# Splitting each 128x520 output tile of a hybrid decoder layer into a pass of high weights and a pass of low weights

## The chip, the cores and the metric

The kernel runs on one core of a Trainium2 chip. The metric is device time in microseconds (us) of one execution, the median of several runs. TensorE (PE) multiplies, with its weight loads told apart as PEld; VectorE is DVE, ScalarE ACT, GpSimd POOL; SyncE (SP) issues most of the transfers.

## The reference, cut to what matters

One decoder layer is computed for 512 prompt tokens and 8 sample tokens together (520 columns), with a final norm. Nearly all the work is nine matrix products in float32:

```python
z = xn @ w_in                       # q, k, v, o, ig, fg, u, vb, ga, gb
y_a = (jax.nn.sigmoid(o) * h) @ w_a
y_b = spatial_gate(u, vn, w_s, b_s) @ w_b
x = x + (jax.nn.sigmoid(ga) * y_a + jax.nn.sigmoid(gb) * y_b) @ w_o
up = rmsnorm(x, g2) @ w_up          # then a causal convolution of width 3
x = x + (jax.nn.silu(a) * gval) @ w_down
```

## The kernel before, in words

**Split products.** A float32 weight W is split into a high part (`whi`, rounded by ACT into the type float32r) and a low part (`wlo` = W - whi, by DVE), and so is each activation (`xh`, `xl`). A product W x is then three products: whi xh, whi xl and wlo xh.

**Slots and tiles.** The weights come in 149 slots of 128x1024 (those of the last product, `w_down`, of 128x1024 or 128x896). Slot by slot, SP loads into `raw` (two buffers), ACT's `split` (its activations all have line 427) makes `whi` and raises `w_hi`, DVE's `low` (line 748) makes `wlo` and raises `w_lo`. `whi` and `wlo` have two buffers each; ACT takes one again when the tile that read it has raised `done`. On PE one call of `tile` (lines 1318 to 1338) works through a slot: 8 k tiles (7 in some of `w_down`), and for each the three products for both column halves of 260: 6 matmuls a k tile, 48 a tile. The matmul itself is line 1316 (`MM`). The two halves lie in the two banks of `out_ps[p]`, which is emptied (`evac`) by ACT or DVE before the tile after next may begin. The last slot group (output tile 7 of `w_down`, 132 matmuls) isn't done by `tile` but by `last_tile` (line 1502), half by half.

**What a tile waits for.** At its start: `w_lo` of its slot, and the emptied bank. Four tiles also have `each`: before the products of k tile k they wait until k+1 tiles of their activation have been made. These are `S_GATE` (the gates, on `s_xu`, from DVE line 770), `S_Q` (on `s_xn`, DVE line 791), `S_WO` (the first tile of w_o, on `s_m`, from DVE line 1077: `ml`) and `S_UP` (the first of w_up, on `s_x2`, DVE line 1090: `x2l`). In `S_WO` and `S_UP` the eighth activation tile comes out of the tile of PE that ran just before: ACT or DVE read its bank, DVE makes the next `wlo`, a high part is made by ACT and the low part by DVE.

**Work in the middle of a tile.** `mid` is called after the products of k tile `mid_at`; it issues transposes, or the products of another part, or sums over partitions. Those that the prediction speaks of are `square_sums` (lines 1351 to 1356, in slot `S_VB + 1`, `mid_at=0`), whose sum leads through ACT's square root and DVE's reciprocal (line 786) to `scaled_vb` (line 799), which empties the bank for `S_VB + 2`; and `norm_sums` (lines 1474 to 1479, in `S_UP`, `mid_at=5`), which takes POOL's sums of squares (lines 1290 to 1294).

The rule of order in the four `each` tiles stands in these lines:

```python
for k in range(nk):
    if each is not None:
        pe.wait_ge(each, k + 1)
```

Of the kernel before, what the change touches and what calls it, by code (L numbers as in the profile page):

```python
# [23 lines left out]
P = 128  # L24
# [5 lines left out]
HALF = TOK // 2  # L30
# [47 lines left out]
def hybrid_layer(nc, ins, outs):  # L78
    with ExitStack() as ctx:
# [5 lines left out]
        def at(name, shape, offset, dt=F32):  # L85

            return nc.alloc_sbuf_tensor_at(name, shape, dt, offset=base + offset)
# [4 lines left out]
        def sem(name):  # L92
            return ctx.enter_context(nc.semaphore(name))
# [70 lines left out]
        whi = [at(f"whi{t}", [P, KT * P], R0 + 8192 + 4096 * t, F32R) for t in range(2)]  # L164
        wlo = [at(f"wlo{t}", [P, KT * P], R0 + 16384 + 4096 * t, F32R) for t in range(2)]
# [101 lines left out]
        w_hi = sem("w_hi")  # L267
        w_lo = sem("w_lo")
# [1045 lines left out]
        def _(pe):  # L1314
            def MM(*a, **k):
                return pe.matmul(*a, **k)  # L1316

            def tile(n, hi, lo, k0=0, nk=KT, bank=None, use=None, start=True, stop=True, mid=None, mid_at=3, each=None, end=None):

                p = n.c % 2  # L1320
                pe.wait_ge(w_lo, n(1))
                if start:
                    pe.wait_ge(evac[p if bank is None else bank], n.half(1) if use is None else use)
                o = out_ps[p if bank is None else bank]
                for k in range(nk):
                    if each is not None:
                        pe.wait_ge(each, k + 1)
                    w = slice(k * P, (k + 1) * P)
                    for wt, x in ((whi[p], hi), (whi[p], lo), (wlo[p], hi)):
                        for a in range(2):  # L1330
                            m = MM(o[:, a, 0:HALF], wt[:, w], x[:, k0 + k, a * HALF:(a + 1) * HALF],
                                   start=start and k == 0 and wt is whi[p] and x is hi,
                                   stop=stop and k == nk - 1 and wt is wlo[p])
                    if k == mid_at and mid is not None:
                        mid()
                m.then_inc(done, 1)
                if end is not None:
                    end()

            def transposes(b, evn, vb=None):  # L1340

                if vb is None:
                    evacuated(pe, evn)
                else:
                    pe.wait_ge(s_vbg, vb + 1)
                pe.wait_ge(tre[b.c % 2], b.half(1))
                for c in range(NC):
                    m = pe.transpose(trp[b.c % 2][:, c, :], ftmp[b.c % 2][:, c * P:(c + 1) * P], ident[:, :])  # L1348
                m.then_inc(tr_done, 1)
# [13 lines left out]
            for _ in range(WARM):  # L1363
                MM(aux[:, 0, 0:P], ones[:, :], ones[:, :], start=True, stop=True)
            tile(At(S_GATE), xuh, xul, each=s_xu)
            tile(At(S_VB), xuh, xul)
            tile(At(S_VB + 1), xuh, xul, mid_at=0, mid=square_sums)
            pe.wait_ge(s_tri, 1)
            tile(At(S_VB + 2), xuh, xul, mid_at=4, mid=lambda: vb_transposes(0), end=lambda: vb_transposes(1))
# [59 lines left out]
            with pe.Fori(1, 4) as i:  # L1429
                for t in range(2):  # L1430
                    tile(At(S_V + t, i, 2), xh, xl,
                         mid=lambda: transposes(At(B_V + t - 1, i, 2), At(S_V + t - 1, i, 2)))
# [182 lines left out]
```

## Time and profile before

| | us |
|---|---|
| median of 3 runs (lowest, highest) | 921.11 (920.89, 921.35) |
| the profiled execution | 922.31 |
| its span in the trace | 919.8 |
| PE busy in the span | 905.6 (98%) |
| PE weight loads busy | 900.7 (98%) |
| DVE busy | 529.1 (58%) |
| ACT busy | 365.1 (40%) |
| POOL busy | 135.6 (15%) |

The span is what the trace covers; the device time of the same execution is 2.5 us longer. Busy times of PE count a matmul from its start to its modelled end, and matmuls overlap, so the pace of PE is read from the starts of rows and their counts, not from the mean of one. In the timeline a row that says x2 is two matmuls (the two column halves), and its start is that of the first.

### The profile page before, as it was taken

To read this page: it belongs to the slowest core of one execution; us is meant where nothing else is said; L and a number is where in the kernel's file an instruction comes from. 1 tells how busy PE (TensorE), PEld (TensorE's weight loads), DVE (VectorE), ACT (ScalarE), POOL (GpSimd) and SP (SyncE) were. 2 spreads that over 40 slices of the span, in tenths; PEclk is the share of its full clock that TensorE was granted. 3 is DMA by queue.
4 is the path that set the end of the run, shared out by engine and by line. 5 is a ranking of instruction groups with operands and counts; after the bars stand their busy time and mean duration, and the time that the engine had idled before them with its cause. 6 is when DMAs were issued, how large, how long until landed. Compare 5 with 4: busy or idle time off the path is not lost.

```text
span 919.8 us, 19638 instructions
## 1 busy us (share of the span) xinstructions
PE 905.6 (98%) x7442; PEld 900.7 (98%) x7442; DVE 529.1 (58%) x811; ACT 365.1 (40%) x553; POOL 135.6 (15%) x182
## 2 busy tenths in 40 slices
PE   9999999999999999999999999999999999999995
PEld 9999999999999999999999999999999999999995
DVE  7877565443884444333346777777777777323235
ACT  7653334544863323222223344444444444222231
POOL 0871000002541111000016500000000000000002
PEclk9999999999999999999999999999999999999998
DMA  5332432234862222532233222222222222332322
GB/s 208 109 99 93 138 137 102 85 101 156 300 249 69 69 74 86 175 100 91 91 111 81 93 87 92 91 91 91 91 91 91 91 91 90 103 94 86 97 69 93
DMA packets 30187, 100.21 MB, mean 109 GB/s; under 512 B 4524, under 2 KB 6604, under 8 KB 29896
## 3 DMA queue, kind: packets, MB, share of 16 engines
q1 hardware_dynamic: 28672, 93.99, 30.7%
q0 software_dynamic: 1328, 5.72, 2.3%
q8 instruction: 24, 0.39, 0.2%
q14 instruction: 11, 0.09, 0.0%
q10 hardware_dynamic: 152, 0.02, 0.0%
HBM read 92.37 MB, written 7.35 MB: 108 GB/s over the span
## 4 chain that ended last, share of the span: by engine, by line
PE 92%; POOLq 3%; issue 2%; DVE 1%; DMA 1%; POOL 1%; ACT 0%; DVEq 0%; SPq 0%; ACTq 0%
PE out L1316 86%; PE aux L1316 2%; PE trp L1316 2%; POOLq L1293 2%; POOLq L1291 1%; PE trp L1348 1%; DMA raw<-in_w_dn 0%; PE aux L1454 0%; DMA cwb<-in_conv_wb 0%; DVE y L1177 0%; POOL out_conv_old L1277 0%; DVE ftmp L1173 0%; POOLq L1284 0%; DVE wlo L748 0%; POOL sconv L1285 0%
## 5 line engine op out<-in xcount | busy, mean ns | idle before, releaser
L748 DVE TENSOR_TENSOR wlo<-raw,whi 128x1024 fp32r<-128x1024 f32 (+1 forms) x148 | 188.4, 1273 | 207.5 <-ACT whi L427 207.2
L427 ACT ACTIVATE whi<-raw 128x1024 fp32r<-128x1024 f32 (+1 forms) x148 | 155.4, 1050 | 253.0 <-PE out L1316 251.3
L1316 PE MATMUL out<-xh,whi 128*128 128x260 f32 x768 | 158.7, 288 | 0.0
L1316 PE MATMUL out<-xh,wlo 128*128 128x260 f32 x768 | 154.6, 283 | 0.0
L1316 PE MATMUL out<-xl,whi 128*128 128x260 f32 x768 | 154.3, 282 | 0.0
L1316 PE MATMUL out<-x2h,wlo 128*128 128x260 f32 x704 | 141.9, 283 | 0.0
L1316 PE MATMUL out<-x2h,whi 128*128 128x260 f32 x704 | 141.8, 282 | 0.0
L1316 PE MATMUL out<-x2l,whi 128*128 128x260 f32 x704 | 141.6, 283 | 0.0
L1316 PEld LDWEIGHTS out<-xh,whi 128*128 128x128 f32 x768 | 118.7, 189 | 0.5
L1316 PEld LDWEIGHTS out<-xh,wlo 128*128 128x128 f32 x768 | 118.3, 188 | 0.0
L1316 PEld LDWEIGHTS out<-xl,whi 128*128 128x128 f32 x768 | 118.2, 188 | 0.0
L1316 PEld LDWEIGHTS out<-x2h,whi 128*128 128x128 f32 x704 | 108.6, 188 | 0.1
L1316 PEld LDWEIGHTS out<-x2h,wlo 128*128 128x128 f32 x704 | 108.5, 188 | 0.0
L1316 PEld LDWEIGHTS out<-x2l,whi 128*128 128x128 f32 x704 | 108.2, 188 | 0.0
L1316 PE MATMUL out<-acth,whi 128*128 128x260 f32 x338 | 70.7, 283 | 1.6 <-DVE wlo L748 1.6
L1316 PE MATMUL out<-acth,wlo 128*128 128x260 f32 x338 | 70.6, 283 | 0.0
L1316 PE MATMUL out<-actl,whi 128*128 128x260 f32 x338 | 70.4, 283 | 0.0
L1112 DVE TENSOR_TENSOR up<-out,rbc 128x520 f32<-128x520 f32 x44 | 30.9, 701 | 42.3 <-PE out L1316 42.2
L1316 PEld LDWEIGHTS out<-acth,whi 128*128 128x128 f32 x338 | 53.1, 188 | 1.9 <-DVE wlo L748 1.8
L1316 PEld LDWEIGHTS out<-acth,wlo 128*128 128x128 f32 x338 | 53.1, 188 | 0.0
L1316 PEld LDWEIGHTS out<-actl,whi 128*128 128x128 f32 x338 | 53.0, 188 | 0.0
L1299 POOL COPY nconv<-up 128x10 f32 x44 | 8.9, 203 | 242.9 <-DVEq L1113 242.9
(266 smaller groups left out, 1397.9 us busy)
## 6 DMA issues: line engine op xcount, KB each, us to landing
raw<-in_w_slots SPq DMA_DIRECT2D x125, 512.0 KB, 3.3
raw<-in_w_dn SPq DMA_DIRECT2D x16, 448.0 KB, 3.3
c_ring<-in_C_state SPq DMA_DIRECT2D x8, 512.0 KB, 4.6
row<-scratch SPq DMA_DIRECT2D x8, 512.0 KB, 5.5
out_C_sample<-c_ring SPq DMA_DIRECT2D x8, 512.0 KB, 4.2
raw<-in_w_dn SPq DMA_DIRECT2D x8, 512.0 KB, 3.5
x<-in_x_all SPq DMA_DIRECT2D x4, 520.0 KB, 6.2
xres<-in_x_all POOLq DMA_DIRECT2D x1, 2080.0 KB, 11.4
```

The lines of the kernel that those rows point to most:

```text
L427: return act.activation(out, in_, func, **kw_)
L748: TT(wlo[p][:, 0:width], raw[p][:, 0:width], whi[p][:, 0:width].bitcast(F32), ALU.subtract)\
L1112: TT(both(up[t][:, 2:2 + TOK]), out2(n), both(rbc2[:, :]), ALU.mult).then_inc(evac[n.c % 2], 1)
L1291: pool.drain()
L1293: pool.drain()
L1299: pool.tensor_copy(nconv[:, i * 2 + t, :], up[t][:, SEQ:2 + TOK]).then_inc(s_nc, 1)
L1316: return pe.matmul(*a, **k)
L1348: m = pe.transpose(trp[b.c % 2][:, c, :], ftmp[b.c % 2][:, c * P:(c + 1) * P], ident[:, :])
```

## The change

Inside `tile` the order is turned: the outer loop is now over the two weight parts, the inner over the k tiles. The first pass has 4 matmuls a k tile (whi with the high and the low activation), 32 in all, and carries the waits of `each`; the second has 2 a k tile (wlo with the high activation), 16 in all. The tile's start waits for `w_hi`, and `w_lo` is waited for ahead of the second pass. `mid` is called at the place in the new order that is nearest to where it was, by number of matmuls.

```diff
             def tile(n, hi, lo, k0=0, nk=KT, bank=None, use=None, start=True, stop=True, mid=None, mid_at=3, each=None, end=None):
 
                 p = n.c % 2
-                pe.wait_ge(w_lo, n(1))
+                pe.wait_ge(w_hi, n(1))
                 if start:
                     pe.wait_ge(evac[p if bank is None else bank], n.half(1) if use is None else use)
                 o = out_ps[p if bank is None else bank]
-                for k in range(nk):
-                    if each is not None:
-                        pe.wait_ge(each, k + 1)
-                    w = slice(k * P, (k + 1) * P)
-                    for wt, x in ((whi[p], hi), (whi[p], lo), (wlo[p], hi)):
-                        for a in range(2):
-                            m = MM(o[:, a, 0:HALF], wt[:, w], x[:, k0 + k, a * HALF:(a + 1) * HALF],
-                                   start=start and k == 0 and wt is whi[p] and x is hi,
-                                   stop=stop and k == nk - 1 and wt is wlo[p])
-                    if k == mid_at and mid is not None:
-                        mid()
+                for q, wt in enumerate((whi[p], wlo[p])):
+                    if q == 1:
+                        pe.wait_ge(w_lo, n(1))
+                    for k in range(nk):
+                        if each is not None and q == 0:
+                            pe.wait_ge(each, k + 1)
+                        w = slice(k * P, (k + 1) * P)
+                        for x in ((hi, lo), (hi,))[q]:
+                            for a in range(2):
+                                m = MM(o[:, a, 0:HALF], wt[:, w], x[:, k0 + k, a * HALF:(a + 1) * HALF],
+                                       start=start and q == 0 and k == 0 and x is hi,
+                                       stop=stop and q == 1 and k == nk - 1)
+                        if mid is not None and (q, k) == (((0, (3 * mid_at + 2) // 2), (1, 3 * mid_at + 2 - 2 * nk))[3 * mid_at + 2 >= 2 * nk]):
+                            mid()
                 m.then_inc(done, 1)
```

How the instructions move is shown at two places on PE. The first is the end of `S_WO`, the first tile of w_o, where `mh` and `ml` are the high and low parts of the merged branches and `merged_lo` is the semaphore that `ml` raises. Before:

```order
L1316 MATMUL out1<-mh_62,whi1_113 128x260 [waits merged_lo]
L1316 MATMUL out1<-mh_62,whi1_113 128x260
L1316 MATMUL out1<-ml_63,whi1_113 128x260 x2
L1316 MATMUL out1<-mh_62,wlo1_115 128x260 x2
L1316 MATMUL out0<-mh_62,whi0_112 128x260 [waits bank_emptied0,w_lo]
```

Now:

```order
L1316 MATMUL out1<-mh_62,whi1_113 128x260 [waits merged_lo]
L1316 MATMUL out1<-mh_62,whi1_113 128x260
L1316 MATMUL out1<-ml_63,whi1_113 128x260 x2
L1316 MATMUL out1<-mh_62,wlo1_115 128x260 [waits w_lo]
L1316 MATMUL out1<-mh_62,wlo1_115 128x260 x15
L1316 MATMUL out0<-mh_62,whi0_112 128x260 [waits bank_emptied0,w_hi]
```

The wait for the eighth `ml` had 42 matmuls of the tile ahead of it and 6 behind; now it has 28 ahead and 20 behind. The same holds in the other `each` tiles.

The second place is the start of slot `S_VB + 1`, where `square_sums` issues two matmuls into `aux` for the sum of squares of x (`xsum`). Before:

```order
L1316 MATMUL out0<-xuh_57,whi0_112 128x260 [waits bank_emptied0,w_lo]
L1316 MATMUL out0<-xuh_57,whi0_112 128x260
L1316 MATMUL out0<-xul_58,whi0_112 128x260 x2
L1316 MATMUL out0<-xuh_57,wlo0_114 128x260 x2
L1316 MATMUL aux<-xsum_54,ones 128x260 [waits square_sum_ready]
```

Now:

```order
L1316 MATMUL out0<-xuh_57,whi0_112 128x260 [waits bank_emptied0,w_hi]
L1316 MATMUL out0<-xuh_57,whi0_112 128x260
L1316 MATMUL out0<-xul_58,whi0_112 128x260 x2
L1316 MATMUL out0<-xuh_57,whi0_112 128x260 x2
L1316 MATMUL out0<-xul_58,whi0_112 128x260 x2
L1316 MATMUL aux<-xsum_54,ones 128x260 [waits square_sum_ready]
```

The sums stood behind 6 matmuls of the tile and stand behind 8. (In `S_VB + 2` a transpose moves in the same way from behind 30 matmuls to behind 32; the other calls of `mid` keep their number.) DVE, ACT and SP keep their order of instructions throughout.

## Rows read from the trace of the kernel before

**Rows 1.** The page, busy times with their shares of the span.
```profile
span 919.8 us, 19638 instructions
...
PE 905.6 (98%) x7442; PEld 900.7 (98%) x7442; DVE 529.1 (58%) x811; ACT 365.1 (40%) x553; POOL 135.6 (15%) x182
```

**Rows 2.** The chain that ended last, in order of time: start, length, what.
```profile
384.68 92.29 PE out L1316 x768
...
901.90 6.12 PE out L1316 x51
```

**Rows 3.** Waits of PE: us in total, times, longest.
```profile
PE out L1316 <- DVE wlo L748: 1.6, 1, 1.6
...
PE out L1316 <- DVE ml L1077: 0.6, 1, 0.6
```

**Rows 4.** Timeline of PE in S_WO: start, length, operation [idle before <-releaser].
```profile
476.80 0.40 PE L1316 MATMUL out<-mh,whi 128*128 128x260 f32 x2
...
482.56 0.51 PE L1316 MATMUL out<-mh,whi 128*128 128x260 f32 x2 [0.56 <-DVE ml L1077]
482.90 0.40 PE L1316 MATMUL out<-ml,whi 128*128 128x260 f32 x2
...
483.39 0.41 PE L1316 MATMUL out<-mh,whi 128*128 128x260 f32 x2
```

**Rows 5.** Timeline of DVE in the same stretch.
```profile
481.12 1.39 DVE L1077 TENSOR_TENSOR ml<-merged,mh  x1 [0.92 <-ACT mh L427]
```

**Rows 6.** Timeline of PE in S_UP.
```profile
523.75 0.40 PE L1316 MATMUL out<-x2h,whi 128*128 128x260 f32 x2
...
528.29 1.15 PE L1316 MATMUL aux<-acc,ones 128*128 128x260 f32 x4
529.08 0.60 PE L1316 MATMUL out<-x2h,whi 128*128 128x260 f32 x2
...
530.72 0.40 PE L1316 MATMUL out<-x2h,whi 128*128 128x260 f32 x2
```

**Rows 7.** Timeline of DVE and POOL in the same stretch.
```profile
526.95 1.80 DVE L1090 SCALAR_TENSOR_TENSOR x2l<-x,gains,x2h  x1
...
534.78 0.70 DVE L1112 TENSOR_TENSOR up<-out,rbc 128x520 f32<-128x520 f32 x1
...
526.09 2.10 POOL L1292 TENSOR_TENSOR acc<-acc,sqa 128x520 f32<-128x520 f32 x1
```

**Rows 8.** Timeline around S_GATE, and the line of the xl tiles.
```profile
8.65 4.11 DVE L770 SCALAR_TENSOR_TENSOR xul<-x,gains,xuh 128x520 fp32r<-128x520 f32 x6
...
8.93 0.49 PE L1316 MATMUL out<-xuh,whi 128*128 128x260 f32 x2
...
L791 DVE SCALAR_TENSOR_TENSOR xl<-x,gains,xh x8: 758/1374/1804, 33.7 to 61.8; 128x520 fp32r<-128x520 f32 x8
```

**Rows 9.** Timeline of PE, ACT and DVE from square_sums to the start of S_VB + 2.
```profile
21.28 1.04 PE L1316 MATMUL aux<-xsum,ones 128*128 128x260 f32 x4
...
22.36 0.69 ACT L427 ACTIVATE rbc<-aux,eps 128x520 f32<-128x520 f32 x1 [0.48 <-PE aux L1316]
...
23.08 3.40 DVE L786 RECIPROCAL rbc<-rbc 128x520 f32<-128x520 f32 x1
26.58 1.53 DVE L799 TENSOR_TENSOR ftmp<-out,rbc 128x520 f32<-128x520 f32 x2
...
26.96 0.41 PE L1316 MATMUL out<-xuh,wlo 128*128 128x260 f32 x2
...
27.43 0.48 PE L1316 MATMUL out<-xuh,whi 128*128 128x260 f32 x2
```

**Rows 10.** Timeline of PE's weight loads in the warm-up, up to the first tile.
```profile
1.20 5.88 PEld L1316 LDWEIGHTS aux<-ones 128*128 128x128 f32 x31 [1.20 <-DVE ones L762]
...
6.89 2.09 PEld L1316 LDWEIGHTS aux<-ones 128*128 128x128 f32 x18
```

**Rows 11.** Windows: stretch, length, busy PE, PEld, DVE, ACT, POOL, granted clock, DMA share, GB/s.
```profile
894.00:898.00 4.00, 3.64 (x30) 3.64 (x31) 1.62 (x3) 2.75 (x4) 0.00 (x0) 1.00 0.00 0
```

## The prediction

> **What bounds the kernel now.** I read the page's busy times first, then the chain that ended last, then PE's waits, and then the timeline around each tile that waits for its activations. PE is busy for 905.6 of 919.8 us [rows 1], and the chain shows how evenly: 768 matmuls in 92.29 us, 120.2 ns each, over 16 whole tiles with all their starts and loop ends [rows 2]. So PE's issue order sets the time, and only two things can change it: the pace of a matmul, and the moments when PE stands still. Of the latter PE's waits hold few: 1.6 us for a `wlo` and 0.6 us for `ml` [rows 3]. In the timeline a wait costs somewhat more than its listed idle time, because the row behind it also starts late: in `S_WO` the pairs follow at 0.34 us instead of 0.24 once [rows 4].
>
> **What the change removes.** The wait for `w_lo` at a tile's start becomes one for `w_hi`, which comes earlier. That is worth something only where a tile's start was late on `wlo`. The one listed wait on `wlo`, 1.6 us, is near the end, in `last_tile`, which the change doesn't touch; its loads, splits and `done` counts keep their order, so it stays. The tiles before it show none. I take 0 us, with 0 also as the bound of the gain: the 16 tiles of [rows 2] begin without any loss. The number of matmuls and weight loads (7442 each [rows 1]) is unchanged, and DVE, ACT and SP issue what they issued.
>
> **What the change adds, one.** A wait for `w_lo` in the middle of each of 146 tiles. By then `wlo` has been there longer than it was at the tile's start before, so the wait itself is over. Whether a wait that is over breaks the flow between matmuls isn't shown for this place. Lower bound 0: the same kind of wait at the tile starts of [rows 2] costs nothing. Upper bound: what a real wait adds behind it, 0.10 us (0.34 less 0.24 [rows 4]), 146 times, 14.6 us. I take 0, since the tile start is the nearest row by far.
>
> **What it adds, two: the `each` tiles.** The eighth activation tile is needed after 28 matmuls instead of 42, that is 14 x 0.120 = 1.68 us sooner, and the second pass can't be used to cover for it, since it stands behind. I go through the four.
>
> `S_WO` starts at 476.80 and the next tile at 483.39 [rows 4]: 6.59 us for 48 matmuls that take 48 x 0.120 = 5.77, so 0.82 us are lost now. `ml` ends at 481.12 + 1.39 = 482.51 [rows 5], and that moment hangs on the end of the tile ahead of `S_WO` (its bank, its `wlo`, `mh`), not on `S_WO` itself. PE will be at the eighth k tile at 476.80 + 28 x 0.120 = 480.16 and stand until 482.56. Since it already stands now, all of the 14 matmuls add to it: **+1.68 us**. Bounds 1.4 to 2.0.
>
> `S_UP` starts at 523.75. Its last `x2l` runs from 526.95 to 528.75, stretched beside POOL's addition, which ends at 528.19 [rows 7]; so far PE needed it only after the norm sums, at about 530.0, and lost nothing to it. The new order needs it at 523.75 + 3.36 = 527.11. With the 0.05 us from the end of `ml` to the next start and the 0.10 us of restart, as in `S_WO`, PE goes on as if at 528.90: 1.79 us lost. What it loses now goes away in return: the tile takes 530.72 - 523.75 = 6.97 us [rows 6], of which 5.77 are its matmuls and 4 x 0.22 = 0.88 the sums, so 0.32 us go to the wait for POOL, and after a stand of 1.79 us POOL is long done. Net **+1.47 us**. The lower bound is 0.4, if `x2l` should come as quickly as the 0.75 us that POOL leaves it elsewhere (the shortest of the like operation `xl` took 0.758 [rows 8]); the upper bound is 1.8. The row itself is taken, because POOL and DVE both start from the same `x1` as before. Next in line is the reciprocal chain that frees the bank for the tile after next: it was done at 534.78 + 0.70 = 535.48 [rows 7] and needed at 530.72 + 5.77 = 536.49, 1.0 us of cover. The norm sums move with the stand (36 matmuls are ahead of them in both orders), so the cover stays.
>
> `S_GATE` starts at 8.93, right behind the warm-up, whose last weight load ends at 6.89 + 2.09 = 8.98 [rows 8, 10], so the earlier `w_hi` gives nothing. The six last `xul` end between 9.4 and 8.65 + 4.11 = 12.76, one each 0.68 us. Today PE takes 0.72 us a k tile and is behind them; in the first pass it takes 0.48 and overtakes them. It would be at the eighth at 8.93 + 3.36 = 12.29 and goes on as if at 12.76 + 0.15 = 12.91: **+0.62 us**, bounds 0.4 and 0.9 (several short stands instead of one).
>
> `S_Q` costs nothing: the last `xl` starts at 61.8 [rows 8] and none took over 1.8 us, and its k tile is needed at about 67.
>
> **What it adds, three: `mid` moved.** `square_sums` stands 2 matmuls later, 0.24 us. Behind it is a chain: ACT's root at 22.36, DVE's reciprocal from 23.08, `scaled_vb` from 26.58, and PE starts `S_VB + 2` at 27.43 although its pairs were due at 26.96 + 0.24 = 27.20 [rows 9]. So this chain ends last there already, by 0.23 us, and the shift goes through: **+0.21 us** (a little of it is hidden behind the `wlo` that DVE makes ahead of the reciprocal), bounds 0 and 0.3. The transpose in `S_VB + 2` comes 0.24 us later and nothing waits for it soon; 0, bounds 0 and 0.2.
>
> **Sum.** 1.68 + 1.47 + 0.62 + 0.21 = 3.98 us, on a span of 919.8 and an execution of 922.31, which gives 923.8 and 926.3. The profiled execution lies 1.2 us above the median of the runs, 921.11; carried over to that, 925.1 us, +0.43%. The likely case's own bounds are 2.2 (1.4 + 0.4 + 0.4 + 0) and 5.2 (2.0 + 1.8 + 0.9 + 0.3 + 0.2).
>
> **Rivals.** *A: the order itself makes matmuls faster (not slower than before).* If part of the 120.2 ns were paid for changing between high and low operands, the second pass, with `wlo` and the high activation alone, could run quicker. There are 6924 matmuls in `tile`, so 3.98 / 6924 = 0.57 ns less for each, 0.5% of the pace, is the point from which the change isn't slower; twice that gives 917 us. Against it: `last_tile` has yet another order (whi, whi, wlo in one half, always the same bank) and runs 51 matmuls in 6.12 us, 120.0 ns [rows 2]; the pace doesn't react to the order. The Trainium skill, TensorE: Matmul & The Clock Gate, Back-to-back issue gap, gives a matmul of N columns N / 2.4 + 2.5 ns, an estimate of 110.8 ns for 260; the trace has 120.2. Were the new order to reach that figure, 6924 x 9.4 ns = 65 us would go; nothing in the trace points to it.
>
> *B: the middle wait breaks the flow.* 146 times 0.10 us, 14.6 us: 939.7 us. Against it speaks that tile starts are free; for it only that no row shows the place itself.
>
> *C: the long stand in `S_WO` costs speed afterwards.* At the start PE's weight loads took 5.88 / 31 = 0.190 us each, and later 2.09 / 18 = 0.116 [rows 10]; that slow stretch cost 31 x 0.074 = 2.3 us. If a stand of 2.4 us brought it back, the time would be 927.4 us. After the stand of 1.6 us in `last_tile` the granted clock was 1.00, 2.4 GHz [rows 3, 11], and `S_UP`'s stand is about as short. A stand of 2.4 us doesn't occur in the trace. The Trainium skill, same page, Why this matters for your kernels, warns that a pause between matmul bursts sends the clock to its lower level if it is long enough; this would be that case, and no row here shows where it begins.
>
> *D: the stands are absorbed.* If `ml` and `x2l` came sooner than in the trace, or each stand only replaced another further on, under 1.8 us would be left: 922.5 us. Against it: after `S_UP` the chain is PE without a wait until `last_tile`, so nothing further on can give the time back.
>
> **Chances.** The sum 0.79; A 0.06; B 0.05; C 0.06; D 0.04. What a measurement of this kernel can tell from no change is 0.2%, 1.84 us. The sum, B and C are slower: 0.90. A lies half beyond the other edge and half within, D within: faster 0.03, same 0.07. The predicted time is the sum's, 925.1 us. The range takes the sum's bounds, 923.3 to 926.3, and reaches upward to take in C: 923.2 to 927.5; A, B and D are left out, 0.15.
>
> **What would show it.** PE's waits would name `ml` with about 2.2 us in place of 0.6, `x2l` with about 1.6 (new), and `xul` with some tenths (new); POOL's 0.3 would be gone; the `wlo` wait would stay at 1.6 in `last_tile` and appear in no tile. `S_WO` would take 8.3 us from its start to the next tile, `S_UP` 8.4. Matmuls would go on at 120.2 ns, in both passes and over the pass boundary. The prediction is wrong if the pace moves by over 0.5 ns, if the pass boundary shows a gap, or if the two stands together are under 1.5 us.

## The result, and the profile after

The changed kernel takes 923.99 us (median of 6 runs, 923.23 to 925.66) against 921.23 us (920.89 to 921.42): 1.003 times the time before, with a 95% interval of 1.002 to 1.004. That is 2.76 us more, slower, where 3.98 us more were forecast. The profiled execution took 924.2 us with a span of 922.3 us.

The page of the changed kernel, busy times, against [rows 1]:

```profile
span 922.3 us, 19638 instructions
...
PE 904.8 (98%) x7442; PEld 899.0 (97%) x7442; DVE 525.7 (57%) x811; ACT 365.2 (40%) x553; POOL 135.9 (15%) x182
```

The span grew by 2.5 us while PE's busy time fell by 0.8: the loss is idle time. The fall in busy time is no measure of the pace of the matmuls, because the warm-up matmuls alone took 7.01 us in this execution and 7.97 in that of the kernel before. PE's waits of the changed kernel (total, times, longest), against [rows 3]:

```profile
PE out L1316 <- DVE ml L1077: 2.2, 1, 2.2
PE out L1316 <- DVE x2l L1090: 1.5, 1, 1.5
PE out L1316 <- DVE wlo L748: 1.4, 1, 1.4
PE aux L1316 <- DVE ones L762: 1.2, 1, 1.2
PE aux L1316 <- ACT sqa L427: 0.5, 1, 0.5
PE out L1316 <- DVE ftmp L799: 0.3, 1, 0.3
PE out L1316 <- DVE xul L770: 0.3, 1, 0.3
```

The wait for `ml` has grown from 0.6 us to 2.2, and those for `x2l` and `xul` are new. The wait for `scaled_vb` (`ftmp`) has become long enough to be listed. The one for `wlo` is still the one in `last_tile`, and no other tile waits for a `wlo`, neither at its start nor in its middle.

The timeline of PE in `S_WO` (start, length, operation, idle before it), against [rows 4]:

```profile
477.11 0.41 PE L1316 MATMUL out<-mh,whi 128*128 128x260 f32 x2
...
482.83 0.51 PE L1316 MATMUL out<-mh,whi 128*128 128x260 f32 x2 [2.21 <-DVE ml L1077]
...
483.42 2.08 PE L1316 MATMUL out<-mh,wlo 128*128 128x260 f32 x16
485.34 0.41 PE L1316 MATMUL out<-mh,whi 128*128 128x260 f32 x2
```

DVE there, against [rows 5]:

```profile
481.43 1.35 DVE L1077 TENSOR_TENSOR ml<-merged,mh  x1 [0.91 <-ACT mh L427]
```

`ml` starts 4.32 us after the tile's start, as before (481.12 - 476.80), so it hangs on the tile ahead. The tile now takes 485.34 - 477.11 = 8.23 us instead of 6.59. All 16 matmuls of `wlo` stand behind the late part and can't cover for it.

PE in `S_UP`, against [rows 6], and DVE, against [rows 7]:

```profile
525.66 0.41 PE L1316 MATMUL out<-x2h,whi 128*128 128x260 f32 x2
...
530.70 0.51 PE L1316 MATMUL out<-x2h,whi 128*128 128x260 f32 x2 [1.52 <-DVE x2l L1090]
...
531.77 1.04 PE L1316 MATMUL aux<-acc,ones 128*128 128x260 f32 x4
...
534.09 0.41 PE L1316 MATMUL out<-x2h,whi 128*128 128x260 f32 x2
```

```profile
528.87 1.77 DVE L1090 SCALAR_TENSOR_TENSOR x2l<-x,gains,x2h  x1
```

8.43 us instead of 6.97, and the sums (`aux`) no longer wait for POOL. At the start of the kernel (PE, against [rows 8, 9]) there are several short stands in `S_GATE`, and `S_VB + 2` starts at 28.18 instead of 27.43. With the shorter warm-up PE began `S_GATE` at 7.96 instead of 8.93, and overtook `xul` the sooner:

```profile
7.96 0.49 PE L1316 MATMUL out<-xuh,whi 128*128 128x260 f32 x2
...
9.46 0.51 PE L1316 MATMUL out<-xuh,whi 128*128 128x260 f32 x2 [0.29 <-DVE xul L770]
...
12.81 0.51 PE L1316 MATMUL out<-xuh,whi 128*128 128x260 f32 x2
...
25.52 0.40 PE L1316 MATMUL out<-xul,whi 128*128 128x260 f32 x2
25.76 2.10 PE L1316 MATMUL out<-xuh,wlo 128*128 128x260 f32 x16
...
28.18 0.48 PE L1316 MATMUL out<-xuh,whi 128*128 128x260 f32 x2 [0.32 <-DVE ftmp L799]
```

The rows at 25.52 and 25.76 are the last pair of a first pass and the first pair of its second: they follow at 0.24 us, as pairs do inside a pass, so the wait for `w_lo` at this boundary leaves no gap.

Last, the chain in order of time. The first row answers to [rows 2]; the second is the stretch from the norm sums of `S_UP` to just ahead of the last stand, 2958 matmuls:

```profile
385.10 92.18 PE out L1316 x768
...
532.81 354.86 PE out L1316 x2958
```

The first took 92.29 us before. The second took 355.40 us before, as this row of the kernel before shows:

```profile
529.44 355.40 PE out L1316 x2958
```

So a matmul of this stretch takes 119.97 ns instead of 120.15. Where the time went, by the start of the same tile in the two traces:

| moment | before | after | shift | of it new |
|---|---|---|---|---|
| `S_VB + 2` starts | 27.43 | 28.18 | +0.75 | +0.75 |
| `S_WO` starts | 476.80 | 477.11 | +0.31 | -0.44 |
| the tile behind `S_WO` starts | 483.39 | 485.34 | +1.95 | +1.64 |
| `S_UP` starts | 523.75 | 525.66 | +1.91 | -0.04 |
| the tile behind `S_UP` starts | 530.72 | 534.09 | +3.37 | +1.46 |
| PE goes on in `last_tile` | 894.36 | 896.93 | +2.57 | -0.80 |

The stands cost 0.75 + 1.64 + 1.46 = 3.85 us. The pace gives back 0.44 + 0.04 + 0.54 (355.40 - 354.86) = 1.02 us, and 0.26 us of the last row is a shorter wait for `wlo` (idle 1.37 us instead of 1.63), behind a last transfer that took 3.55 us instead of 3.80.

The 0.75 us of the first row is the least certain of these. Of it 0.52 us are in `S_GATE` (the next tile starts at 15.31 instead of 14.79) and 0.23 in `S_VB + 1`, whose sums moved (7.11 us from its start to that of `S_VB + 2`, instead of 6.88). But the start moves between executions too. In the eight profiles whose kernels have the old order in these tiles and the pace of the kernel before or of two passes, `S_VB + 2` starts anywhere from 27.28 to 27.99, with warm-ups of 7.0 to 8.5 us.

### The profile page after: what moved, and what is told of

It is laid out like the page before. It is cut to its first block, busy times and chain, and to the rows that moved or that the text cites. A ratio compares the mean times of both kernels' runs of the same rounds, so it can differ in the third digit from the quotient of the medians.

```text
span 922.3 us, 19638 instructions
## 1 busy us (share of the span) xinstructions
PE 904.8 (98%) x7442; PEld 899.0 (97%) x7442; DVE 525.7 (57%) x811; ACT 365.2 (40%) x553; POOL 135.9 (15%) x182
## 4 chain that ended last, share of the span: by engine, by line
PE 95%; DVE 2%; ACT 1%; DMA 1%; DVEq 0%; issue 0%; ACTq 0%; SPq 0%
PE out L1316 90%; PE trp L1316 2%; PE aux L1316 2%; PE trp L1351 1%; DMA gains<-in_gains 0%; DVE wlo L748 0%; DMA raw<-in_w_dn 0%; PE aux L1457 0%; DVE rbc L786 0%; ACT whi L427 0%; DVE y L1177 0%; DVE x2l L1090 0%; DVE ftmp L1173 0%; DVE ml L1077 0%; ACT xuh L427 0%
## 5 line engine op out<-in xcount | busy, mean ns | idle before, releaser
L748 DVE TENSOR_TENSOR wlo<-raw,whi 128x1024 fp32r<-128x1024 f32 (+1 forms) x148 | 185.5, 1254 | 208.3 <-ACT whi L427 208.0
L1316 PE MATMUL out<-xh,wlo 128*128 128x260 f32 x768 | 100.5, 283 | 0.0
L1316 PEld LDWEIGHTS out<-xh,wlo 128*128 128x128 f32 x768 | 95.8, 189 | 0.0
L1316 PE MATMUL out<-x2h,wlo 128*128 128x260 f32 x704 | 92.8, 284 | 0.0
L1316 PEld LDWEIGHTS out<-x2h,wlo 128*128 128x128 f32 x704 | 88.3, 189 | 0.1
L1316 PE MATMUL out<-acth,wlo 128*128 128x260 f32 x338 | 49.0, 283 | 0.0
L1316 PEld LDWEIGHTS out<-acth,wlo 128*128 128x128 f32 x338 | 44.1, 188 | 0.0
```

Source lines behind the costliest of these rows:

```text
L748: TT(wlo[p][:, 0:width], raw[p][:, 0:width], whi[p][:, 0:width].bitcast(F32), ALU.subtract)\
```

## The experiments

**Are the pace and the stands what they seem? Four runs.** First the kernel before once more, unchanged:

> The kernel before, unchanged, for a second profile. Pace theory (the two-pass order runs 0.15% quicker a matmul): the chain's 2958 matmuls of the w_up and w_down stage take 355.4 us again, within 0.1. Noise theory (the pace differs by as much from one execution to the next, whatever the order): the same stretch lies somewhere between 354.8 and 355.9.

Measured, in the chain of that run:

```profile
529.34 355.40 PE out L1316 x2958
```

355.40 us again, so the pace of this stretch has no noise worth the name. Then the changed kernel once more:

> The changed kernel again. Pace theory: the stretch of w_up and w_down takes 354.9 us within 0.1, and the stands are 2.2 us on ml and 1.5 us on x2l as before. Noise theory: the stretch is off 354.9 by 0.3 or more. The median is 924 us; if the spread of over 2 us between executions comes from the clock after the long stand, a profile of a longer execution shows matmuls after 483 us at a slower pace or a granted clock under 1.00.

It took 924.06 us (ratio 1.0033, 1.0022 to 1.0043), the waits were the same 2.2 and 1.5 us, and the stretch took

```profile
532.61 354.82 PE out L1316 x2958
```

The gain in pace is real: 0.18 to 0.20 ns a matmul in this stretch. Between the two second profiles the same sums come out: the stands cost 1.67 us in `S_WO` and 1.44 in `S_UP`, and the pace gives back 1.06. Only `S_GATE` differs. In the changed kernel's second profile the warm-up took 8.38 us, PE began `S_GATE` at 9.34, didn't catch up with `xul` (the last ended at 12.60) and took 5.82 us for the tile (to 15.16), which is no loss at all; the two kernels' `S_VB + 2` are still 0.63 us apart (28.03 against 27.40), 0.24 of it from the moved sums and the rest from the later start. Three of the changed kernel's 14 timed executions lay above 925 us (925.3 to 926.57); the profile caught none of them, so what they lost stays open.

The next run takes the stands away and keeps the two passes elsewhere:

```diff
-                for q, wt in enumerate((whi[p], wlo[p])):
+                if each is not None or mid_at == 0:
+                    pe.wait_ge(w_lo, n(1))
+                    for k in range(nk):
...
+                else:
+                    for q, wt in enumerate((whi[p], wlo[p])):
```

> The changed kernel, with the five tiles that wait for their activations or carry the first sums (S_GATE, S_Q, S_WO, S_UP, S_VB+1) back in the old order, k tile by k tile. Theory of the stands (they cost 0.75 + 1.64 + 1.46 = 3.85 us and the pace gives 1.1 back): 920.1 us, slightly under the kernel before, ml's wait at 0.6 and none on x2l. Rival (the order of all tiles costs something and the stands only moved the loss): 922 us or more.

920.49 us, ratio 0.9991 (0.9982 to 1.000), with `ml` at 0.6 and no wait on `x2l`. Its stretch:

```profile
529.55 354.83 PE out L1316 x2958
```

So two passes in the tiles that wait for nothing cost nothing and gain a little: 0.8 us between the medians, an interval that just reaches no change, and 1.0 us in the profile (0.42 between the starts of `S_VB + 2` and `S_WO`, 0.57 in the stretch above). The whole loss lies in the five tiles. The converse, the condition turned round (`each is None and mid_at != 0` for the old order):

> The kernel before, with only those five tiles in two passes. Theory of the stands: 921.2 + 3.85 = 925.1 us, and the pace of the w_up and w_down stretch stays 120.15 ns a matmul. Rival (the stands cost less than counted and the pace of the other 141 tiles isn't involved): 924 us, as the changed kernel.

925.54 us, ratio 1.0044 (1.003 to 1.0058), 4.2 us more than the 921.3 of the same chip. That fits the theory of the stands (925.1) better than the rival (924). The stretch is back at the old pace:

```profile
533.04 355.39 PE out L1316 x2958
```

In its profile `ml` took only 0.70 us, not 1.35, and the wait was 1.6 us:

```profile
482.27 0.70 DVE L1077 TENSOR_TENSOR ml<-merged,mh  x1 [0.91 <-ACT mh L427]
```

POOL issues a transfer at that moment, once the constants that it waits for have landed. In this run and in the changed kernel:

```profile
482.22 2.07 POOL L1277 DMA_DIRECT2D out_conv_old<-cst  x1 [2.73 <-DMA cwb<-in_conv_wb]
...
481.28 2.07 POOL L1277 DMA_DIRECT2D out_conv_old<-cst  x1 [2.63 <-DMA cwb<-in_conv_wb]
```

The issue began 0.05 us ahead of `ml` here, and 0.15 us ahead in the changed kernel (481.28 against 481.43). All fourteen profiles of this case fall in line. In the four where the issue began at most 0.11 us ahead, `ml` took 0.70 us. In the ten where it began 0.12 us or more ahead, `ml` took 1.20 to 1.39 and ended 1.49 to 1.52 us after the issue's start. So the moment at which those constants land decides over 0.5 to 0.7 us of this stand, in either order; why isn't shown. The cost of the change in `S_WO` doesn't depend on it: with `ml` at 0.70 the tile took 7.60 us here and 5.91 in the old order (the run below with the weights' places exchanged), a difference of 1.69. `S_VB + 2` started at 28.62 in that profile, 1.19 us later than in the kernel before.

**What is the pace made of? Four runs of one execution each.** The four edits, the first of the weights' places and the others of the inner loops. Three start from the kernel before; the three passes replace the two passes of the run with the five tiles in the old order:

```diff
-        whi = [at(f"whi{t}", [P, KT * P], R0 + 8192 + 4096 * t, F32R) for t in range(2)]
-        wlo = [at(f"wlo{t}", [P, KT * P], R0 + 16384 + 4096 * t, F32R) for t in range(2)]
+        whi = [at(f"whi{t}", [P, KT * P], R0 + 16384 + 4096 * t, F32R) for t in range(2)]
+        wlo = [at(f"wlo{t}", [P, KT * P], R0 + 8192 + 4096 * t, F32R) for t in range(2)]
```

> The kernel before, with the places of whi and wlo in SBUF exchanged, order and all else the same. Address theory (a matmul's pace depends on where in SBUF its operands lie relative to those read beside it, which is why the same order gives the same pace to 0.01 us in every execution): the w_up and w_down stretch of 2958 matmuls leaves 355.40 us by at least 0.1, either way. Order theory (what counts is only how often high and low operands alternate): 355.40 again within 0.02.

```diff
-                    for q, wt in enumerate((whi[p], wlo[p])):
+                    for q, (wt, x) in enumerate(((whi[p], hi), (whi[p], lo), (wlo[p], hi))):
```

> As the run with the five tiles in the old order, but all other tiles in three passes: whi with the high activation over all k tiles, whi with the low one, wlo with the high one. Order theory (each change between high and low operands costs something): fewer changes still than with two passes, so the stretch takes less than 354.83 us, some 354.5. Address theory: no direction follows, it lies between 354 and 356.5.

```diff
-                    for wt, x in ((whi[p], hi), (whi[p], lo), (wlo[p], hi)):
-                        for a in range(2):
+                    for a in range(2):
+                        for wt, x in ((whi[p], hi), (whi[p], lo), (wlo[p], hi)):
```

> The kernel before, with the two column halves as the outer and the three products as the inner loop inside a k tile, as in the last tile: more changes of weights (4 a k tile instead of 2). Order theory: slower than 355.40 us for the 2958 matmuls. Address theory: no direction follows. A pace that depends only on the number of matmuls: 355.40 again.

```diff
-                    for wt, x in ((whi[p], hi), (whi[p], lo), (wlo[p], hi)):
+                    for r, (wt, x) in enumerate(((whi[p], hi), (wlo[p], hi), (whi[p], lo))):
```

> The kernel before, with the three products inside a k tile in the order whi xh, wlo xh, whi xl (instead of whi xh, whi xl, wlo xh). If the pace comes from the number of consecutive matmuls on one weight tile (runs of 2 in place of 4 and 2): slower than 355.40 us for the 2958 matmuls. If it comes from the moving operand changing between xh and xl: the same number of changes, 355.40. If it comes from how the addresses of neighbouring accesses fall together, no direction follows.

The same stretch in the chains of the four: weights swapped,

```profile
529.00 355.40 PE out L1316 x2958
```

three passes,

```profile
527.96 354.00 PE out L1316 x2958
```

half by half,

```profile
528.26 353.87 PE out L1316 x2958
```

and `wlo` second:

```profile
529.65 355.40 PE out L1316 x2958
```

Three things follow for this stretch. Exchanging the places of the weights changes nothing, so the theory of addresses has fallen as far as this exchange goes. The number of changes between operands isn't it either: three passes have the fewest and half by half the most, and both are quicker than the rest; by the theory that each change costs something, half by half was to be slower. And the length of the runs on one weight tile isn't it: `wlo` second has runs of 2 only and keeps 355.40. What is left is that the order of the same matmuls moves the pace, by up to 0.52 ns or 0.4% (1.53 us over 2958), and by nearly the same in each execution that was repeated.

The pace of one stretch isn't that of the kernel, though. Two other stretches, from a tile's start to that of a later one, in the same profiles:

| stretch, in the kernel before | before | two passes | three passes | half by half |
|---|---|---|---|---|
| 187.92 to 225.08, six tiles of v | 37.16 | 37.15 | 37.12 | 37.24 |
| 271.06 to 380.12, fifteen tiles of `S_BY` | 109.06 | 109.18 | 109.01 | 108.90 |
| the 2958 matmuls | 355.40 | 354.86 | 354.00 | 353.87 |

Two passes are the slowest order in the second row, and half by half in the first. The other profiles with these orders repeat the figures of the first two rows within 0.02 us. Both stretches hold other work of PE between the products (transposes, and the products of the recurrent state). Whether that or the operands makes the difference wasn't tested, nor was the place of the activations; why the order matters is open. The spans were 917.0 us with three passes and 917.2 us half by half, against 919.8 and 919.4 for the kernel before.

**Rival C, a long stand.** The kernel before, with all eight `ml` awaited at the start of `S_WO`:

```diff
                 pe.wait_ge(w_lo, n(1))
+                if each is s_m:
+                    pe.wait_ge(s_m, KT)
```

> The kernel before, with S_WO waiting for all eight ml at its start. It stands from the tile's start until ml is there, 5.86 us instead of 0.82 lost, so 5.04 us more: 926.3 us. Rival C of the prediction (a long stand brings a slow stretch of the clock): the granted clock falls under 1.00 behind the stand and the matmuls up to some us later are slower, up to 2.3 us more, 928.6 us.

928.39 us, ratio 1.0078 (1.0061 to 1.0095). Windows of that run (length, busy PE, granted clock, DMA share, GB/s):

```profile
474.00:478.00 4.00, 2.79 (x24) 1.00 0.39 131
478.00:480.00 2.00, 0.00 (x0) 0.68 0.74 222
480.00:482.00 2.00, 0.00 (x0) 0.50 0.79 264
482.00:484.00 2.00, 1.60 (x7) 0.50 0.36 21
484.00:486.00 2.00, 2.00 (x13) 0.61 0.97 45
486.00:488.00 2.00, 2.00 (x19) 1.00 0.40 27
```

and PE behind the stand (its releaser isn't named; by the edit it is the last `ml`):

```profile
482.40 0.77 PE L1316 MATMUL out<-mh,whi 128*128 128x260 f32 x2 [5.61 <-issue]
482.97 0.64 PE L1316 MATMUL out<-ml,whi 128*128 128x260 f32 x2
...
485.14 0.60 PE L1316 MATMUL out<-mh,whi 128*128 128x260 f32 x2
...
489.66 0.40 PE L1316 MATMUL out<-mh,whi 128*128 128x260 f32 x2
```

During the stand of 5.61 us the granted clock fell to 0.50, 1.2 GHz, and came back while PE was busy again: the first 12 matmuls took 485.14 - 482.40 = 2.74 us instead of 1.44, and the tile's 48 took 7.26 us (to 489.66) instead of 5.77. The stand that was counted on (5.04 us more) and these 1.49 us make 6.5 of the 7.3 us between the medians; the other 0.8 us isn't explained. The Trainium skill, TensorE: Matmul & The Clock Gate, Why this matters for your kernels, says that idle gaps between bursts of matmuls bring the clock down; this trace agrees, with 0.50 in the rows above. In the changed kernel, with a stand of 2.21 us, it didn't happen (the same windows of its profile):

```profile
480.00:482.00 2.00, 0.62 (x6) 1.00 0.67 262
482.00:484.00 2.00, 1.17 (x9) 1.00 0.19 78
```

**A version that beats both.** Since the stands and the pace are separate, each can be had alone. First, on top of the five tiles in the old order, the late part goes to the very end of `S_WO`, and the norm sums of `S_UP` a k tile later:

```diff
-                        pe.wait_ge(each, k + 1)
+                        pe.wait_ge(each_hi if last else each, k + 1)
...
+                    for r, (wt, x) in enumerate(((whi[p], hi), (wlo[p], hi), (whi[p], lo)) if last else
+                                                ((whi[p], hi), (whi[p], lo), (wlo[p], hi))):
+                        if last and r == 2:
+                            pe.wait_ge(each, k + 1)
...
-            tile(At(S_WO), mh, ml, each=s_m)
+            tile(At(S_WO), mh, ml, each=s_m, each_hi=s_mh)
...
-            tile(At(S_UP), x2h, x2l, each=s_x2, mid_at=5, mid=lambda: norm_sums(s_acc, 1, s_ss2))
+            tile(At(S_UP), x2h, x2l, each=s_x2, mid_at=6, mid=lambda: norm_sums(s_acc, 1, s_ss2))
```

> The run with the five tiles in the old order, and in S_WO the eighth k tile issues whi mh and wlo mh as soon as mh is there and whi ml last; the norm sums in S_UP stand behind 42 matmuls instead of 36. Theory of the stands: mh is there at 4.2 us into S_WO, before it is needed, and ml 0.34 us after the four matmuls instead of 0.82, so 0.5 us less; POOL's sums are there before they are needed, so another 0.3 less: 0.8 us under the run with the old tiles, 919.7 us. Rival (the norm sums' chain is the next to be late): no more than 0.5 less.

919.62 us, ratio 0.9985 (0.9976 to 0.9994), 0.87 us under the run with the five tiles. That run was on another chip, where the kernel before took 0.34 us more, so the medians can't tell 0.8 us from the rival's 0.5. The profiles can: `S_WO` took 6.06 us instead of 6.58 and `S_UP` 6.64 instead of 6.98, 0.86 us together, as forecast. The wait on `ml` is off the list. Then the order of two splits near the end, on ACT and likewise on DVE:

```diff
-                    if last and s == 2:
-                        split_last()
                     split(n.plus(2), (DN_CUTS[w + 1] - DN_CUTS[w]) * P)
+                    if last and s == 2:
+                        split_last()
```

> The run before this one, and near the end the split of slot 147 ahead of that of the last slot, on ACT and DVE, so that it no longer waits for the last transfer. Theory: the wait of 1.4 to 1.6 us on wlo in the last tile goes, 1.5 us less, 918.2 us. Rival (the last slot's split, now later, becomes late for PE, or the first half's sums are): the wait only moves to a later slot.

918.06 us, ratio 0.9971 (0.9958 to 0.9983), 1.56 us less. The wait on `wlo` that both kernels have before the last tile's second slot came from the order of two splits and is gone. What its list still has of `wlo` is at the very start, in `S_GATE`, where this execution's warm-up ended early:

```profile
PE out L1316 <- DVE wlo L748: 0.6, 1, 0.6
```

And all of it with the half-by-half order in every tile:

> All that paid, together: every tile k tile by k tile with the column halves outside and the three products inside, the eighth k tile of S_WO with ml last, the norm sums behind 42 matmuls, and slot 147 split ahead of the last. If pace and waits add up: the run with the two passes and the same waits took 918.1 us, and half by half runs 353.87 against 354.83 us for 2958 matmuls, 0.325 ns each, over 6924 matmuls 2.25 us: 915.8 us. Rival (a quicker PE only waits longer for wlo or the banks): 917 to 918 us, with longer waits of PE.

916.31 us, ratio 0.9944 (0.993 to 0.9957), 0.5 us above the sum (915.8) and 5.2 us under the kernel before on the same chip (921.47). Its whole list of PE's waits:

```profile
PE aux L1316 <- DVE ones L762: 1.2, 1, 1.2
PE aux L1316 <- ACT sqa L427: 0.5, 1, 0.5
```

The rival, that a quicker PE only waits longer, has fallen: no wait of PE has grown. The sum counted 0.325 ns for each of 6924 matmuls, 2.25 us. From the start of `S_VB + 2` to the end of the span this run took 1.66 us less than the one before it (914.5 - 27.90 against 915.7 - 27.44), which fits the table above: half by half doesn't gain in every stretch what it gains in that of the 2958.

## Why the prediction was right, and where it was off

- **What bounds the kernel:** right. PE's issue order does, and the idle time that grew is that in front of the four late operands.
- **The wait at the tile's start gives nothing:** right. No tile waited for a `wlo` in the two traces that are compared. In the second profile of the kernel before, whose warm-up ended sooner, `S_GATE` stood 0.6 us for its `wlo`; two passes don't gain that either: the changed kernel, after a warm-up as short, began `S_GATE` 0.93 us sooner than that profile (7.96 against 8.89), and ended it 0.54 us later (15.31 against 14.77), because `xul` is later still. The run with the five tiles in the old order gained only what its pace explains, the 1.0 us above.
- **A second wait in each of 146 tiles costs nothing:** right, rival B has fallen. The boundary shows no gap (25.52 to 25.76), and with that wait in every tile the matmuls of the stretch are quicker, not slower.
- **`S_WO` +1.68:** measured +1.64. **`S_UP` +1.47:** measured +1.46, the wait for POOL gone as worked out. Of `ml` the prediction says that its end hangs on the tile ahead alone. It also hangs on POOL's issue, and that `ml` took 1.35 us again, and not 0.70, was luck for the wait of 2.2 us, though not for the difference.
- **`square_sums` +0.21:** measured +0.23 and +0.24 in the two profiles of the changed kernel.
- **`S_GATE` +0.62:** right in its mechanism, but the size depends on when the warm-up ends and when `xul` does, both of which the prediction took from one trace. It was +0.52 in the changed kernel's first profile (start 7.96, last `xul` at 12.76) and nothing in its second (9.34 and 12.60). In the run with only the five tiles in two passes it was +0.89 (8.88 and 13.06; 6.75 us for the tile instead of 5.86). That the stands together were forecast at 3.98 us and measured 3.85 is in this part luck.
- **The pace unchanged:** this step was off. The argument was that 51 matmuls of `last_tile`, in another order, ran at 120.0 ns against 120.2, and that this meant no reaction. But 0.15 ns over 51 matmuls is 0.008 us, less than the last digit of that row, so it couldn't have shown a change of this size; over 6924 matmuls it is 1 us. Nor did the order of `last_tile` tell how that order does elsewhere: half by half ran at 119.63 ns in the stretch of 2958. The pace gave back 1.02 us. That is rival A's mechanism at a quarter of the size from which it would have decided.
- **The wait for `wlo` stays at 1.6:** it stays, but its length hangs on the last transfer: 1.37 us here, 1.3 to 1.8 in the other profiles that have it. The 0.26 us that this gave back weren't forecast.
- **Rival C** was a true mechanism in the wrong range: it needs a longer stand than the change makes in the profiled execution. Whether it explains the three slow executions of the changed kernel isn't known.
- **Rival D**, that the stands are absorbed, has fallen: the run with only the five tiles in two passes shows them whole at the end (4.2 us).

The three parts add to 3.85 - 1.02 - 0.26 = 2.57 us at `last_tile`, 2.5 us in the span and 2.76 us between the medians. So the forecast of 3.98 us was 1.2 us too high: the pace, which was put at nothing, is most of that.

## What to carry to other kernels

Where an engine is busy throughout, an operand that arrives late should be used last: count how much of the consumer's work stands ahead of the wait and how much behind, since reordering moves the wait by that difference (14 matmuls, 1.68 us worked out and 1.64 measured). A reordering that is good for most tiles can be bad for the few that follow their producer closely; give these an order of their own. And compare long stretches by their count of matmuls, 355.40 against 354.86 us over 2958: a tenth of a nanosecond in the pace is read off there and not off a short row. Do it for each stage: the order that is quicker in one can be slower in another. And look at the start in more than one execution before a cost there is counted to a tenth of a microsecond.

## What the runs showed of the hardware that was not expected

The pace of a stream of matmuls with a weight load each repeats to 0.01 us in 355 between two executions of the kernel before (to 0.04 between two of the changed one), and yet depends on the order of the same matmuls. In the stretch of 2958 it was 120.15 ns k tile by k tile, 119.97 in two passes, 119.68 (354.00 / 2958) in three, 119.63 (353.87 / 2958) half by half. Moving the weights to each other's place left it at 120.15. In two other stretches the orders ranked otherwise (109.06 us k tile by k tile against 109.18 in two passes). The cause was not found. A stand of 5.61 us let the granted clock fall to 0.50 and cost about 1.5 us of slow matmuls behind it; stands of up to 2.21 us left it at 1.00 in the profiles. A DVE operation of 0.70 us with two inputs (`ml`) took 1.20 to 1.39 us in all ten profiles in which POOL's issue of a transfer, 2.07 us long, had begun 0.12 us or more ahead of it, and 0.70 in all four in which it had begun at most 0.11 us ahead.
